# Wide first weight pieces in k order, split first projections, and block 0 transposed on TensorE

## What is computed

```python
h = RMSNorm(x) * g_pre
u = h @ w_in                      # 1024 x 4096, eight segments of 512 columns
rq, rk, rv, rg, hq, hf, hi, hg = split(u, 8)
# heads 0..3: retention, rotary q and k, a decay gamma per head
# heads 4..7: f = lb + (1-lb)*sigmoid(hf); k = 1-f; q = silu(hq); gated recurrence
o = concat(silu(rg) * headnorm(o_ret), silu(hg) * headnorm(o_hgrn))
x = x + RMSNorm(o @ w_out) * g_post
```

## Time and profile before

| what | value |
|---|---|
| time of three runs, median (lowest, highest) | 418.58 us (417.88, 419.2) |
| the profiled execution | 421.18 us |
| its span on core 1, the slowest | 419.6 us |
| spans of the eight cores | 410.7 to 419.6 us |
| TensorE busy | 350.5 us, 84% |
| VectorE, GpSimd, ScalarE busy | 270.9, 211.8, 155.0 us |
| DMA, bytes moved | 54.12 MB, 129 GB/s over the span |
| mean granted TensorE clock | 0.950 on core 1, 0.959 on cores 0 and 6 |

### The profile page before, as it was taken

How to read it: one execution, slowest core, us unless ns; L and a number is a source line. 1 busy time by engine, 2 the same in 40 slices (tenths; PEclk the granted TensorE clock), 3 DMA queues, 4 the chain that set the end, 5 groups by cost and what they waited for, 6 DMA issues and landing times.

```text
span 419.6 us, 7392 instructions; the slowest of 8 cores (410.7 to 419.6 us)
## 1 busy us (share of the span) xinstructions
PE 350.5 (84%) x2065; PEld 173.5 (41%) x2065; DVE 270.9 (65%) x489; ACT 155.0 (37%) x497; POOL 211.8 (50%) x265
## 2 busy tenths in 40 slices
PE   0225498799839799799999997999999999999973
PEld 0211143354424245354544544454545545554531
DVE  0232149845659996969598579739594675764573
ACT  2320022144765235162624444242424344354441
POOL 8501126322767847757475377264476456285130
PEclk9998579899968999999999999999999999999976
DMA  7999999996697528285435773521523534214145
GB/s 157 213 198 157 164 169 166 156 143 129 142 200 183 152 75 199 43 254 112 52 66 162 147 149 97 171 54 27 149 50 117 136 87 116 77 56 97 43 130 166
DMA packets 72118, 54.12 MB, mean 129 GB/s; under 512 B 52240, under 2 KB 61488, under 8 KB 72080
## 3 DMA queue, kind: packets, MB, share of 16 engines
q1 hardware_dynamic: 65744, 43.18, 43.4%
q0 software_dynamic: 6336, 10.49, 17.2%
HBM read 41.73 MB, written 10.09 MB: 123 GB/s over the span
## 4 chain that ended last, share of the span: by engine, by line
PE 73%; DMA 12%; DVE 7%; issue 2%; POOL 2%; ACT 2%; SPq 0%; POOLq 0%; DVEq 0%; ACTq 0%
PE bank L587 41%; PE bank L848 14%; PE bank L574 11%; DMA Wi<-w_in 10%; PE bank L768 2%; PE bank L773 2%; PE bank L785 2%; PE bank L736 2%; DMA ogT<-og 1%; DVE fG L618 1%; DVE tB L653 1%; DVE fR L627 1%; DVE tA L649 1%; POOL Wi L464 1%; DMA QKr<-Ktr 1%
## 5 line engine op out<-in xcount | busy, mean ns | idle before, releaser
L587 PE MATMUL bank<-Wi,xT 128*128 128x512 bf16 (+1 forms) x816 | 193.0, 390 | 11.7 <-DMA Wi<-w_in 5.6
L587 PEld LDWEIGHTS bank<-Wi,xT 128*128 128x128 bf16 (+1 forms) x816 | 80.2, 100 | 107.3 <-issue 22.0
L848 PE MATMUL bank<-Wo,ogT 128*128 128x512 bf16 (+1 forms) x272 | 67.0, 398 | 9.8 <-DMA ogT<-og 4.7
L574 PE MATMUL bank<-xT,Wi 128*128 128x512 bf16 (+1 forms) x320 | 62.5, 343 | 5.3 <-DVE fR L627 2.7
L806 DVE SCALAR_TENSOR_TENSOR og<-bank,rsq,gate 128x128 bf16<-128x128 f32 (+1 forms) x136 | 37.8, 342 | 24.7 <-POOL rsq L803 12.0
L649 DVE TENSOR_TENSOR tA<-bank,rot 128x512 f32<-128x512 f32 (+1 forms) x34 | 23.2, 682 | 37.2 <-PE bank L587 37.2
L852 ACT ACTIVATE og<-bank 128x512 bf16<-128x512 f32 (+1 forms) x34 | 20.4, 601 | 68.3 <-PE bank L848 53.5
L848 PEld LDWEIGHTS bank<-Wo,ogT 128*128 128x128 bf16 (+1 forms) x272 | 26.7, 102 | 43.4 <-issue 17.7
L574 PEld LDWEIGHTS bank<-xT,Wi 128*128 128x128 bf16 x320 | 27.0, 98 | 38.6 <-issue 10.5
L662 POOL TENSOR_TENSOR qtm<-tA,tB 128x512 bf16<-128x512 f32 (+1 forms) x17 | 23.5, 1380 | 37.8 <-DVE tB L653 30.7
L796 ACT ACTIVATE og<-bank 128x128 bf16<-128x128 f32 (+1 forms) x136 | 35.6, 295 | 8.8 <-PE bank L768 7.0
(11 more groups left out here) (94 smaller groups left out, 409.9 us busy)
## 6 DMA issues: line engine op xcount, KB each, us to landing
xr<-xp SPq DMA_DIRECT2D x18, 512.0 KB, 4.5
yp<-xr SPq DMA_DIRECT2D x16, 512.0 KB, 3.1
xs<-xp SPq DMA_DIRECT2D x14, 512.0 KB, 4.4
Wi<-w_in POOLq DMA_DIRECT2D x6, 1024.0 KB, 55.1
Wi<-w_in POOLq DMA_DIRECT2D x4, 512.0 KB, 27.3
Wo<-w_out POOLq DMA_DIRECT2D x2, 1024.0 KB, 83.4
rot<-rot_p SPq DMA_DIRECT2D x16, 96.0 KB, 3.7
gpre<-g_pre SPq DMA_DIRECT2D x1, 512.0 KB, 7.1
```

What stands on the lines that cost most here:

```text
L574: ins = e.matmul(pb(v)[:, 0:nt], lhsT=Wi[:, kc, col0:col0 + 128], rhs=k.xT[:, kc, 0:nt], start=(kc == 0), stop=(kc == 7))
L587: ins = e.matmul(pb(v)[0:L, :], lhsT=k.xT[:, kc, j * 128:j * 128 + L], rhs=Wi[:, kc, seg * 512:(seg + 1) * 512], start=(kc == 0), stop=(kc ...
L848: ins = e.matmul(pb(y)[0:L, :], lhsT=ogT[:, kc, 0:L], rhs=Wo[:, kc, n * 512:(n + 1) * 512], start=(kc == 0), stop=(kc == 7))
```

## The change

- The weight loads: segments 0 and 1 together, as four pieces of two k chunks by 1024 columns; the other segments and `w_out` as before in halves of four k chunks by 1024. Boosts set their order strictly as listed. Completion is tracked per quarter of k.
- `proj_tm` of block 0 for segments 0 and 1 is recorded as four operations of two matmuls, each waiting for its quarter of the weights; they accumulate in the same bank. In block 0 these projections claim only a shared key "first", and not `tA`/`tB`.
- `Kth` and `ogT` of block 0 are transposed on TensorE with a ScalarE copy; the transposing DMAs stay for blocks 1 to 3.
- `g_pre` is given as 128 rows, one per partition, by the host.
- The x tiles of block 1 that are loaded first (two), and the x tiles for `stage_E` of block 0, wait for the last piece of `Wi`.
- `ssx`, `rsx` get four columns; in the first four tiles the squares go to the unused `gate` buffers.
- The chain to `lbc` and the copies of `glT` wait for the fourth norm. `ident` and `mhalf` are made first. A tanh of one column on ScalarE stands at the very start.
- `DMA_RATE` in the planner is 325 instead of 350; boosts of the first x tiles, `gpre` and the first four tiles' `stage_A` are raised.

```diff
-DMA_RATE = 350.0
+DMA_RATE = 325.0
-    g_pre = din("g_pre", [1, 1024])
+    g_pre = din("g_pre", [128, 1024])
...
+        S.op(ACT, lambda e: e.activation(out=warm[:], in_=warm[:], func=AF.Tanh), reads=["warm"], writes=["warm"])
...
-        loads = [(w_in_v, Wi, "Wi", 0, 512, 4), (w_in_v, Wi, "Wi", 512, 512, 4), (w_in_v, Wi, "Wi", 2048, 1024, 4),
-                 (w_in_v, Wi, "Wi", 1024, 1024, 4), (w_in_v, Wi, "Wi", 3072, 1024, 4), (w_out_v, Wo, "Wo", 0, 1024, 4)]
+        loads = [(w_in_v, Wi, "Wi", 0, 2), (w_in_v, Wi, "Wi", 2048, 4), (w_in_v, Wi, "Wi", 1024, 4), (w_in_v, Wi, "Wi", 3072, 4),
+                 (w_out_v, Wo, "Wo", 0, 4)]
...
-                S.ops[wid]["boost"] = 4.0e6 - 1e4 * (nl * 2 + k0 // 4)
+                S.ops[wid]["boost"] = (14.0e6 if wb < 4 else 10.0e6) - 5e5 * wb
+                wb += 1
...
-        gid = S.op(SP, lambda e: e.dma_start(out=gpre[:], in_=g_pre.partition_broadcast(128)), writes=["gpre"], dma_key="gpre")
-        S.ops[gid]["boost"] = 4.95e6
+        gid = S.op(SP, lambda e: e.dma_start(out=gpre[:], in_=g_pre), writes=["gpre"], dma_key="gpre")
+        S.ops[gid]["boost"] = 19.5e6
...
-                    S.ops[xid]["boost"] = 5e6 - 1e5 * i
+                    S.ops[xid]["boost"] = 20e6 - 1e6 * i
+                elif i < 6:
+                    S.ops[xid]["deps"].add(S.last_w[("Wi", 7, 3)])
...
+            if i == 3:
+                first_norms.append(len(S.ops) - 1)
...
+            if i < 4:
+                for o in S.ops[n0:]:
+                    o["boost"] = 9e6 - 1e5 * i
...
+            parts = 4 if (not k.sample and k.b == 0 and seg < 2) else 1
+
+            for q in range(parts):
+                k0, k1 = q * 8 // parts, (q + 1) * 8 // parts
...
+                S.op(PE, mm, reads=WK(seg, k0 // 2, k1 // 2) + [("xT", k.par, j)], writes=[v] + (claim if q == 0 else []))
...
+        def lb_chain():
+            S.op(DVE, lambda e: e.tensor_tensor(out=lbd[:], in0=lbt[:, 0, :], in1=lbt[:, 1, :], op=ALU.subtract),
+                 reads=["lbt"], writes=["lbd"], deps=first_norms)
...
-                     reads=["glT"], writes=[("decS", k.par, c, h) for h in range(4)])
+                     reads=["glT"], writes=[("decS", k.par, c, h) for h in range(4)], deps=first_norms)
...
-                v = proj_tm(k, j, which, [("tA", ts), ("tB", ts)])
+                v = proj_tm(k, j, which, [("tA", ts), ("tB", ts)] if k.sample or k.b else ["first"])
...
-                    if (not k.sample):
+                    if (k.b >= 1 and not k.sample):
...
-                     deps=[sc0[0]])
-            if (not k.sample and not (k.b == 3 and j == 3)):
+                     deps=[sc0[0]] + ([S.last_w[("Wi", 7, 3)]] if k.b == 0 else []))
+            if (k.b >= 1 and not k.sample and not (k.b == 3 and j == 3)):
```

More of the change, by code:

```diff
@@ new lines, in stage_A @@
+            n0 = len(S.ops)
+            junk, jk = (xbf[slot], [("xbf", slot)]) if i >= 4 else (gate[i], [("gate", i, 0), ("gate", i, 512)])
+            sq = i % 4
+            S.op(ACT, lambda e: e.activation(out=junk[0:L, :], in_=xbuf[0:L, :], func=AF.Square, scale=1.0 / 32,
+                                             accum_out=ssx[0:L, sq:sq + 1]),
+                 reads=[xkey], writes=[("ssx", sq)] + jk)
+            S.op(POOL, lambda e: e.tensor_scalar(out=ssx[0:L, sq:sq + 1], in0=ssx[0:L, sq:sq + 1],
@@ L561, in stage_A, with WK @@
                      reads=[T], writes=[("xT", k.par, j)])
-        def WiK(seg):
-            return [("Wi", seg, 0), ("Wi", seg, 1)]
+            if i < 4:
+                for o in S.ops[n0:]:
+                    o["boost"] = 9e6 - 1e5 * i
+        def WK(seg, q0=0, q1=4, nm="Wi"):
+            return [(nm, seg, q) for q in range(q0, q1)]
         def proj_fm(k, col0, seg, claim):
@@ L576, in mm @@
                 return ins
-            S.op(PE, mm, reads=WiK(seg) + [("xT", k.par, j) for j in range(k.ns)], writes=[v] + claim)
+            S.op(PE, mm, reads=WK(seg) + [("xT", k.par, j) for j in range(k.ns)], writes=[v] + claim)
             return v
@@ L850, in mm @@
                     return ins
[L851 removed]
+                S.op(PE, mm, reads=["ogT"] + WK(n, nm="Wo"), writes=[y])
                 S.op(ACT, lambda e, n=n, y=y: e.activation(out=og[0:L, n * 512:(n + 1) * 512], in_=pb(y)[0:L, :], func=AF.Square, scale=1.0 / 32,
@@ L1002 @@
         m["w_out"] = w_out[0]
-        m["g_pre"] = g_pre
+        m["g_pre"] = np.ascontiguousarray(np.broadcast_to(g_pre, (128, D_MODEL)))
         m["g_post"] = g_post
```

62 lines of the change are left out of this document (31 added, 31 removed).

## The result

| | before | after |
|---|---|---|
| median of the runs, us (lowest to highest) | 418.58 (417.88 to 419.20) | 405.98 (405.65 to 408.64) |
| ratio after to before, 95% interval | | 0.9713 (0.9659 to 0.9768) |
| span of the profiled execution, slowest core, us | 419.6 | 404.2 |
| median of the spans of its eight cores, us | 415.5 | 402.6 |

A fourth run of the kernel before, 460.71 us, fell in the slower state that some executions of any kernel show, and is left out. The change makes the kernel 2.9% faster, some 12 us. The forecast was 399.5 us with a range of 391.5 to 411. The slowest cores' spans differ by 15.4 us, but before's slowest core was 4.1 us above the middle one and after's only 1.6, so I read the gain from the medians of the cores: 13.0 us.

The account below looks back on a forecast made before the run. Up to about 80 us the order and rate of the loads bound the kernel, then TensorE. 10.4 + 4.9 + 3.0 − 4.0 + 5.0 = 19.3 us off the span gave 399.5 us, range 391.5 to 411.

Parts of the forecast that it names:

- its own case: The forecast's sum comes through, with or without the gain from g_pre's layout: 393 to 406 us, chance 0.56.
- rival (b): In 112 to 160 us VectorE's serial chain keeps the gain; about half of 19.3 comes through: 409.5 us, chance 0.20.
- Where the loss was: In front of 160 us, with TensorE idle 8.1, 2.9, 4.7 and 8.5 us in four stretches between 31 and 130.
- the four terms: Fourth piece lands at 33.3 us, not 45.2: wide half 6.1, g_pre 2.0, block 1's x tiles 3.1, 4 KB rows 0.7.
- Part 2: Up to 45.3 us: quarter projections run before the fourth piece lands, then VectorE sets the pace; gain 10.4 us.
- Part 3: 45 to 60 us: segments 4 and 5 are there at 45.5 and heads start earlier; gain 4.9 us (bounds 2 and 6).
- Part 4: 60 to 81 us: rotaries done, a head left, TensorE can be full; gain 3.0 of 4.7 us idle.
- Part 5: Front of the kernel: small tables moved behind the norms, worth nothing by itself, only making the split projections possible.
- Part 6: Block 0's transposes on TensorE cost 4.0 us; 112 to 130 us gives back 5.0 (bounds 2 and 9).
- Rival (a): Quarter projections behind the fourth piece run at the lower clock; about 3 us less gain: 402.5 us, chance 0.12.
- Rival (c): Nothing finishes before the fourth piece, which still lands at about 45 us: 425 us; above 418.6 has chance 0.07.
- Rival (d): 4 to 8 us: the slow rate is the queue's start, not g_pre's repeated row; 2 us less gain: 401.5 us.

Follow-up runs that it names:

- e1: Changed kernel with g_pre again as one 4 KB row read for 128 partitions, same order: 407.33 us, ratio 0.9718.
- e5: Changed kernel with x loads of block 1 and stage_E not held behind the last Wi piece: same order 409.87 us, ratio 0.9769; replanned 413.84 us, 0.9851.
- e7: Kernel before with only the wide pieces in k order and the split projections of segments 0 and 1: 412.75 us, ratio 0.9873.
- e2: Changed kernel, same order, but every quarter projection of segments 0 and 1 waits for all four pieces: 414.06 us, ratio 0.9891.
- e6: Changed kernel with a planner model in which SyncE's loads share the rate with the weight pieces instead of queueing behind them: 403.59 us, ratio 0.9597.
- e4: Changed kernel with the copies of glT and the lb chain free of the norms again: 408.43 us, ratio 0.9728.
- e3: Changed kernel with block 0's keys and outputs transposed by DMA from SyncE again, planned anew: 411.21 us, ratio 0.9783.
- e8: Changed kernel, same order, without the filler matmuls on ident in TensorE's idle time: 409.27 us, ratio 0.9738.
- e12: Kernel before with only the planner's model changed, SyncE's loads sharing the rate with the weight pieces: 432.69 us, ratio 1.0348.

## Why the prediction was right, point by point

The time, 405.98 us, lies inside the stated range, but at the outer edge of what the forecast itself gave to its own case (393 to 406) and where rival (b) begins: of the 19.3 us some 13 came.

**Where the loss was**: right. All of the gain lies in front of 130 us, and 160 to 390 us kept its 224 us.

**The landings.** The fourth piece was put at 33.3 us and came at 28.7, so 4.6 us more than the four terms. Right direction, wrong terms. Two of them, 2.0 for `g_pre` and 3.1 for the hold, are worth nothing there: with the repeated row it lands at 28.8 (e1), with the x tiles let go at 28.7 (e5, replanned), and with both at 28.9 (e7). The shape and order of the pieces made all of it, 16.3 us on the slowest cores where the sum gave these 6.8, and some 13 by the medians of the cores (42.0 before); the one late core that I read makes part of the difference. Which of the two, the shape or the order, does it wasn't isolated. That 33.3 was near is in part luck: terms that don't exist stood in for a term that was too small. The hold works on what comes behind: dropping it cost 6 us replanned and perhaps 2 in the same order (e5). Segments 4 and 5 at 42.5 (45.5 foreseen) and the last piece at 72.6 (72.5) are right.

**Part 2, the split**: 10.4 us foreseen; the first feature-major projection is 8.5 us ahead (median of cores), and e2 prices the early quarters alone at 7.4. VectorE set the pace as said, but the rotaries ran from 31.5, not from 33.7. A fifth too high. One sign failed: of the "eight rotaries through by 47" two came at 87.8 and 91.2. Their table is issued by SyncE among the weights; the planner, which puts all transfers in one queue, had them late, and e6, with the other model, has them at 40.6.

**Part 3**: 4.9 foreseen. From 45.3 to 60 us 50 matmuls of 0.216 us are 10.8 us of work against 7.6: 3.2. TensorE waits at each head for the second scan (`fR`, 4.5 us in three times); I had 12.5 us of work there, as though heads followed one another without that.

**Part 4**: 3.0 foreseen, 3.1 found (4.7 less 1.55 idle), though its premise, that the rotaries are done, holds for six of eight.

**Part 5, the tables**: nothing by themselves, right in the changed kernel (e4), and necessary for part 2 in an order that has `glT` ahead of the norms: there no quarter ran before the fourth piece (e7).

**Part 6 is the step that failed**: −4.0 for the transposes and +5.0 for the hand-over to block 1. The transposes are worth having: without them, in an order planned anew, it is 3 us slower (e3), and the DMAs of `ogT` and `Kth` land late. The 5.0 did not come: 81 to 130 us has 8.0 us idle against 8.5 in the earlier trace rows, and 130 to 160 has 2.9 more. I had seen that a hold delays the tiles to 72.5 and took the rest for free; I didn't ask at which place in ScalarE's order the squares would stand. The planner thought these tiles late, and the first two squares ran at 91.7 and 94.3, some 10 and 9 us behind the landing of their tiles; TensorE then waits 4.9 us for `xT` (2.9 to 6.4 over the cores). That is rival (b) in its effect (the hand-over keeps part of the gain) but not in its mechanism: VectorE was busy 13.43 of 18 us there and did not set it. e5 with the same order shows that the first tiles' landing isn't the cause, and e6 that another order loses the wait and gains 1.2%. That the squares' place alone does this wasn't isolated: e6 also has the two late rotary pairs in front and their two banks free, which is a rival of the same weight.

Of the 19.3 us, 12.5 are there at block 1: 1.9 are missing from part 2, 1.7 from part 3, and what is left, some 3.3, from the 5.0; the end agrees with that mark to 0.5 us. These shares are read from marks and stretches, not from a run each.

**Rival (a), the low clock**: it did not come true where it had its price, behind the fourth piece. There TensorE was at the upper clock, from 26.2 us on, ahead of the landing at 28.7. The quarters before 26.2 us did run at half speed, which the prediction put at nothing. That was a little too kind: TensorE has no gap from 23.15 us until the 50 matmuls end, and VectorE's first rotary waits for it (4.31 us, until 31.48). At full speed the 3.9 us in front of 26.2 would have been some 1.9 shorter, an estimate; of this at most 1.1 can reach the first head, since segments 4 and 5 land at 42.5 and it starts at 43.6. No run has quarters at full speed throughout, so this price stays open. The Trainium skill, TensorE: Matmul & The Clock Gate, section HAM oscillation — how this bites in real kernels, asks, for thin matmuls, for all k tiles before a DMA wait; here e2, which runs them all behind the wait, is 7.4 us slower than the split. Its premise, that short bursts between waits fall to the lower clock, agrees with all these traces, with quarters (changed kernel, e8) and with whole projections (e2, until 34.3 us); its advice does not pay here, where work stands ready before the last piece has landed.

**Rival (c)**, slower: its condition, a landing of 39 us or later, did not occur. **Rival (d)** holds in the time, and was inside the forecast.

## What to carry to other kernels

Where an engine waits for a load that comes in pieces, let the consumer start per piece and order the pieces in the order of accumulation; even at half speed the early parts were worth 7.4 us here. Keep loads that nothing needs yet behind the ones that set the pace, but then check where the planned order puts their consumers: an engine in strict order waits for them if they stand too early (14.5 us lost in e12), and the engines behind them wait if they stand too late (4.9 us in the changed kernel). Read a rate, a landing or a span from all cores before it becomes a term of a sum. And check a clock column against the length of a known matmul before reading a clock from it.

## What the runs showed of the hardware

- Loading a repeated 4 KB row into 128 partitions makes the rate in 4 to 8 us differ between cores of one execution by a factor of two (121 to 267 GB/s before, 146 to 293 in e1); with one row per partition the eight cores lie between 238 and 256 GB/s.
- Transfers issued by SyncE beside weight loads issued by GpSimd land late, by an amount that no single rate gives: an x tile of 512 KB took 29.8 us when issued at 42 us among the weights (e12) and 9.0 when issued at 72.7, behind the last of `Wi` (after). A transposing DMA took 32.9 us among them (`xT`, issued at 35.4 us in e12) and up to 10.7 and 12.4 beside the last ones (`ogT`, `Kth` in e3).
- Two matmuls of 512 columns took 1.06 us at the lower clock and 0.59 at the upper; eight transposes 1.01 and 0.61. In the changed kernel, with filler matmuls from 1.9 us on, TensorE got the upper clock at 4.8 to 7.7 us on the eight cores and lost it between 15.3 and 21.9, ahead of or among the first quarters; without fillers (e8) its record begins with the upper clock at 24.0 to 26.9, and the eight transposes before that took 1.01 us each time on the profiled core.
